# The low part of each weight unit made by GpSimd in two operations of 1024 columns instead of one of 2048

## What is computed

```python
f = conv_ffn(u, w_up, conv_w, conv_b, w_down)      # h = conv(u @ w_up); (gelu(gate) * val) @ w_down
p = x @ w_in                                        # GDN, GLA
qkv = causal_conv_silu(p[..., :GDN_QKV], conv_w)
... (o_normed * silu(gate)) @ w_out
x = layer_norm(DEEP_ALPHA * x + y, ln_g, ln_b)
```

## Time and profile before

| | |
|---|---|
| median of 3 runs | 1283.73 us (1282.49 to 1283.79) |
| profiled execution, own time | 1283.86 us |
| its span, first to last instruction | 1282.0 us |
| PE, DVE, ACT, POOL busy | 1216.9, 551.5, 520.3, 378.6 us |
| mean granted clock of TensorE | 0.972 of full speed |

### The profile page before, as it was taken

One profiled execution on the slowest core, in us unless ns is written; L12 is line 12 of the kernel. 1 busy time (PEld: TensorE's weight loads), 2 busy tenths in 40 slices (PEclk: granted clock), 3 DMA queues, 4 the chain that ended last, 5 costly groups with the idle time before them and its releaser, 6 DMA issues.

```text
span 1282.0 us, 16325 instructions
## 1 busy us (share of the span) xinstructions
PE 1216.9 (95%) x6572; PEld 1019.9 (80%) x6572; DVE 551.5 (43%) x853; ACT 520.3 (41%) x669; POOL 378.6 (30%) x92
## 2 busy tenths in 40 slices
PE   5989999999899989999999999999999699999986
PEld 5568878888788867888788978888888479999874
DVE  1464344343722253558854357422100632453714
ACT  4254543445411145654343324644312544335523
POOL 0014433444434433224221120044444124233111
PEclk9889999999999989999999999999999789999998
DMA  9993223222322232223322112032322313222101
GB/s 352 386 323 106 92 83 98 95 91 90 109 94 99 99 125 73 66 50 116 99 66 67 34 33 99 1 93 72 131 99 99 106 33 99 67 66 67 65 1 66
DMA packets 108206, 128.48 MB, mean 100 GB/s; under 512 B 13019, under 2 KB 98785, under 8 KB 108017
## 3 DMA queue, kind: packets, MB, share of 16 engines
q1 hardware_dynamic: 103412, 120.69, 28.2%
q10 hardware_dynamic: 4733, 6.91, 1.6%
HBM read 122.35 MB, written 5.24 MB: 100 GB/s over the span
## 4 chain that ended last, share of the span: by engine, by line
PE 45%; DVE 3%; ACT 1%; issue 1%; DVEq 0%; ACTq 0%
PE ps L242 11%; PE ps L244 11%; PE ps L243 11%; PE ps L1482 2%; PE ps L2064 2%; PE ps L1821 1%; PE ps L1829 1%; PE ps L1858 1%; PE ps L1949 1%; PE ps L1955 1%; PE ps L1950 1%; PE ps L1931 1%; DVE xres L1377 1%; PE ps L2083 1%; DVE xres L1367 0%
## 5 line engine op out<-in xcount | busy, mean ns | idle before, releaser
L364 POOL TENSOR_TENSOR wl<-raw,wh 128x2048 fp32r<-128x2048 f32 x81 | 374.4, 4622 | 875.3 <-ACT wh L389 875.3
L242 PE MATMUL ps<-xth,wh 128*128 128x512 f32 x800 | 321.2, 401 | 3.9 <-DVE xtl L974 3.2
L244 PE MATMUL ps<-xth,wl 128*128 128x512 f32 x800 | 313.6, 392 | 0.0
L389 ACT ACTIVATE wh<-raw 128x2048 fp32r<-128x2048 f32 x81 | 154.9, 1912 | 390.5 <-PE ps L244 390.5
L243 PE MATMUL ps<-xtl,wh 128*128 128x512 f32 x800 | 313.0, 391 | 0.0
L242 PEld LDWEIGHTS ps<-xth,wh 128*128 128x128 f32 x800 | 151.4, 189 | 36.5 <-issue 6.7
L244 PEld LDWEIGHTS ps<-xth,wl 128*128 128x128 f32 x800 | 151.0, 189 | 32.5
L243 PEld LDWEIGHTS ps<-xtl,wh 128*128 128x128 f32 x800 | 151.6, 190 | 29.1
L242 PE MATMUL ps<-wh,xth 128*128 128x256 f32 (+1 forms) x320 | 98.8, 309 | 3.4 <-DVE xtl L867 3.4
L243 PE MATMUL ps<-wl,xth 128*128 128x256 f32 (+1 forms) x320 | 98.0, 306 | 0.0
L244 PE MATMUL ps<-wh,xtl 128*128 128x256 f32 (+1 forms) x320 | 97.8, 306 | 0.0
(11 more groups left out here) (287 smaller groups left out, 1733.1 us busy)
## 6 DMA issues: line engine op xcount, KB each, us to landing
ada<-in_ada_w SPq DMA_DIRECT2D x24, 1024.0 KB, 10.6
raw<-in_gdn_w_in SPq DMA_DIRECT2D x24, 1024.0 KB, 5.1
raw<-in_ffn_w_up SPq DMA_DIRECT2D x22, 1024.0 KB, 5.0
raw<-in_gla_w_in SPq DMA_DIRECT2D x12, 1024.0 KB, 5.0
raw<-in_ffn_w_down SPq DMA_DIRECT2D x11, 1024.0 KB, 4.8
raw<-in_gdn_w_out SPq DMA_DIRECT2D x8, 1024.0 KB, 4.9
raw<-in_gla_w_out SPq DMA_DIRECT2D x4, 1024.0 KB, 5.0
xres<-in_x SPq DMA_DIRECT2D x4, 512.0 KB, 5.2
```

What stands on the lines that cost most here:

```text
L242: nc.tensor.matmul(o, lh, rh, start=first, stop=False)
L244: return nc.tensor.matmul(o, ll, rh, start=False, stop=last)
L364: nc.gpsimd.tensor_tensor(wl[:, s, :], raw[:, s, :], wh[:, s, :].bitcast(f32), ALU.subtract)\
L389: nc.scalar.activation(wh[:, s, :], raw[:, s, :], ACT.Copy).then_inc(hi_done, 1)
```

## The change

`low` makes the difference in two operations of half the columns. Both belong to the same wait on `hi_done`, and only the second raises `unit_split`, so PE and SP are told when the whole unit is split, as before. The bytes read and written are the same.

```diff
@@ -361,8 +361,9 @@
             def low(u, s):
 
                 pool.wait_ge(hi_done, u + 1)
-                nc.gpsimd.tensor_tensor(wl[:, s, :], raw[:, s, :], wh[:, s, :].bitcast(f32), ALU.subtract)\
-                    .then_inc(unit_split, 1)
+                for part in (slice(0, UNIT // 2), slice(UNIT // 2, UNIT)):
+                    rest = nc.gpsimd.tensor_tensor(wl[:, s, part], raw[:, s, part], wh[:, s, part].bitcast(f32), ALU.subtract)
+                rest.then_inc(unit_split, 1)
```

## The result

The changed kernel takes 1276.9 us in the median (6 runs, 1274.8 to 1278.1), the kernel before, timed beside it, 1283.1 us. The ratio is 0.995, with a 95% interval of 0.9935 to 0.9964: 4.6 to 8.3 us faster. I had forecast 1280.6 us and a range whose lower end was 1279.6. The sign is right.

What follows compares the result with a forecast made beforehand. TensorE's queue, busy 95%, and its own waits were taken to bound the kernel. Terms -2.2 - 1.15 + 0.1 + 0.1 = -3.15 us gave 1280.6 us against the median, range 1279.6 to 1284.7.

Steps and rivals of the forecast that it cites:

- the seam: Between GpSimd's two halves, 2.36 us after the low part's start: an already waiting VectorE operation goes in there.
- The rival to which I gave 0.33: At GpSimd's two halves: VectorE waits through both; +0.4 us, 1284.1 us, no change; chance 0.33.
- a late L1446: At 1197.31 us: L1446 asks too late and waits for the second half; -1.9 us, 1281.8 us; chance 0.17.
- The cost d: Each low part: what one GpSimd operation costs whatever its size, taken as 0.1 us, lower end 0.04.
- The upper end of 0.65: Rival of an expensive second GpSimd operation: 0.65 us fixed cost per operation gives +2.7 us, 1286.4 us; chance 0.05.
- The two terms: TensorE's waits for L989 and ahead of L2075 get shorter: gains of 2.2 and 1.15 us.
- The losses at L903 and in the inversion: At 90.59 us and in the diagonal inversion near 618.65: VectorE ends later for the second half, 0.1 us lost each.
- the clock: TensorE's granted clock around idle stretches: about 1 to 2 us either way, no side taken, priced at nothing.
- the two waits: TensorE's idle 3.28 us behind L989, forecast to fall to 1.06, and 2.06 us before L2075, forecast gone.
- the first place: Near 347.80 us: L994 gets through at the half, TensorE's wait for L989 shortens, gain 2.2 us.
- my 3.4 us of waits: Gains forecast near 347.80 and 1197.31 us together, 2.2 and 1.15 us, from shorter TensorE waits.
- the second place: Near 1197.31 us: L1446 gets through at the half, TensorE's wait before L2075 goes, net gain 1.15 us.

Runs made afterwards that it cites:

- The two places alone: Kernel before with two halves only for the two units whose low parts run near 345.6 and 1195 us: ratio 0.9949 (0.9930 to 0.9968).
- all units but those two: Kernel before with two halves for 79 units, one operation for the units near 345.6 and 1195 us: ratio 1.0002 (0.9990 to 1.0013).
- the filled wait: Kernel before with 13 more, thrown-away matrix products inside TensorE's 3.3 us wait for L989: ratio 0.9985 (0.9974 to 0.9997).
- the repeat: The changed kernel run again, unchanged, against the kernel before: ratio 0.9958 (0.9943 to 0.9973).
- the order alone: Kernel before, but in the down projection's first unit TensorE multiplies into the two free banks before waiting for L989: ratio 0.9977 (0.9966 to 0.9988).

## Why the prediction was wrong, step by step

**What VectorE waits for, and the seam:** right. The seam opens, and the time at which VectorE asks decides: 2.2 and 2.3 us after the start it gets in at 2.4, at 2.5 it doesn't; a cut at 768 columns undoes all. The rival to which I gave 0.33, GpSimd keeping VectorE out through both halves, is refuted by the 0.76 us of L995 and the 1.23 of L1447. L1447 asked 2.29 us after the start, so the rival of a late L1446 missed by 0.1 us only; that margin was thin, as I had said.

**The cost d:** 0.1 us said. A pair takes 4.75 us in the up projection where one operation took 4.61, so 0.14. The upper end of 0.65 was far off.

**The two terms:** -2.2 and -1.15 said, -2.17 and -1.23 in the profiles. The losses at L903 and in the inversion, 0.1 each, did not show: L904 lasts 0.75 us in the changed kernel, where it was 0.82, and TensorE's wait behind the inversion is 0.61 us, where it was 0.77. The two places alone and all units but those two add up to the changed kernel.

**The step that failed is the clock.** I wrote: "I have no reason for a side." There was one. Both terms are idle stretches of TensorE that get shorter, and the earlier trace rows show the clock low around idle stretches. In no profile of this study does a fall stand behind one of the two waits when it is short or filled (0 of 7, 0 of 5). I looked at one execution, saw full speed behind the 3.28 us, and priced the clock there at nothing. In other executions of the same code it falls. So a term is missing from the sum: behind the first place 1.9 us (the filled wait, interval 0.4 to 3.3), behind the second about 1.3 (2.6 measured less 1.23, interval 0 to 2.8). With my 3.4 us of waits these make 6.6, against 6.4 measured, and 5.4 in the repeat. The 1.3 is itself a difference of measured times, so the agreement is in part built in; apart from that the term is shown by the mean clock, higher by 0.0031 and 0.0017.

**What stays open.** The chance of a fall at the second place rests on three of eight profiles and on a difference; I did not fill that wait. How large the term is at each place is open too: the filled wait says 0.4 to 3.3 us at the first, the count of falls about 1, and the order alone nothing. The half clock at L2033 was in 2 of the 13 profiles, both of kernels with both waits long; whether that is chance isn't settled.

## What to carry to other kernels

Cutting an operation that holds another engine off pays only where the other asks before the cut, where it is on the path, and where what stands behind it isn't held off in turn. Find these places and cut there; 79 of 81 cuts here did nothing that shows. An idle stretch of TensorE can cost more than its length: ask for the fall of the clock behind it, by the mean clock of many executions and not by one profile, and fill the stretch with work that is needed anyway where it can't be shortened.

## What was not expected of the hardware

A low part of 384, 1024 and 1664 columns took 0.99, 2.40 and 3.71 us, that of 2048 4.61: some 2.1 us for 1000 columns and less than 0.2 us for the operation itself. An operation of VectorE that already waits gets in between two operations of GpSimd that stand back to back in its queue: L995 lasted 0.76 us instead of 2.93, and the pair of GpSimd 5.18 instead of 4.75. In one case, a scaling of 512 columns with a single SBUF input, 0.54 us long elsewhere, took 1.10 us beside 384 columns of GpSimd. And 2.9 us of useless matrix products inside a wait of 3.3 us made the kernel 1.9 us faster (0.4 to 3.3).
